# Modulation quarters on GpSimd: one broadcast multiply and a fold in place of tile-by-tile multiply and add

## What is computed

```python
c_act = jax.nn.silu(c)
mod = c_act @ w_ada[l] + b_ada[l]                      # [1, 6 * 2048]
sh1, sc1, gt1, sh2, sc2, gt2 = jnp.split(mod[:, None, :], N_MOD, axis=-1)
h = _rmsnorm(x, norm1_g[l]) * (1.0 + sc1) + sh1
...
x = x + gt1 * mix
h = _rmsnorm(x, norm2_g[l]) * (1.0 + sc2) + sh2
x = x + gt2 * _conv_ffn(h, w_up[l], conv_w[l], conv_b[l], w_down[l])
# second block, with c_2 and w_ada_2 (3 * 2048 columns)
shift, scale, gate = jnp.split(mod, 3, axis=-1)
```

## Time and profile before

| what | value |
|---|---|
| three runs | 2760.07, 2768.75, 2771.41 us; median 2768.75 |
| profiled execution, span | 2768.1 us |
| its own time | not given apart; the span lies 0.65 us under the median of the runs |
| PE busy | 2643.3 us (95%), granted clock 0.965 |
| DVE busy | 1864.0 us (67%) |
| POOL busy | 1128.9 us (41%), 612 instructions |
| ACT busy | 1082.6 us (39%) |
| DMA | 568.49 MB, mean 205 GB/s |

### The profile page before, as it was taken

How to read it: one execution, slowest core, us unless ns; L and a number is a source line. 1 busy time by engine, 2 the same in 40 slices (tenths; PEclk the granted TensorE clock), 3 DMA queues, 4 the chain that set the end, 5 groups by cost and what they waited for, 6 DMA issues and landing times.

```text
span 2768.1 us, 47948 instructions
## 1 busy us (share of the span) xinstructions
PE 2643.3 (95%) x20992; PEld 2397.8 (87%) x20992; DVE 1864.0 (67%) x2268; ACT 1082.6 (39%) x1255; POOL 1128.9 (41%) x612
## 2 busy tenths in 40 slices
PE   5689989999999999999999999999999999999997
PEld 2268877778999999999999899989988898999996
DVE  1248863267988888888887775576446874786454
ACT  1133422144434444343446443444334444444353
POOL 0293011013899999999991475862000000000001
PEclk7689989899999999999999999999999999999998
DMA  8967647676877777777765776775767665666664
GB/s 314 321 180 187 183 153 256 221 230 191 228 218 240 240 240 240 240 243 244 243 221 138 190 194 201 209 209 171 183 193 187 161 174 179 172 168 168 183 185 120
DMA packets 759185, 568.49 MB, mean 205 GB/s; under 512 B 46497, under 2 KB 645665, under 8 KB 758849
## 3 DMA queue, kind: packets, MB, share of 16 engines
q1 hardware_dynamic: 758976, 565.42, 69.7%
HBM read 563.29 MB, written 2.10 MB: 204 GB/s over the span
## 4 chain that ended last, share of the span: by engine, by line
PE 80%; DMA 6%; POOL 6%; DVE 5%; ACT 1%; issue 1%; SPq 1%; DVEq 0%; POOLq 0%
PE bank L785 15%; PE bank L768 9%; PE bank L769 9%; PE bank L772 9%; PE bank L788 8%; PE bank L752 5%; PE bank L754 5%; PE bank L753 5%; PE bank L1009 2%; DMA ada<-w_ada 2%; PE bank L741 2%; PE bank L821 2%; PE bank L822 2%; PE bank L823 2%; POOL prod_e L625 1%; POOL prod L625 1%
## 5 line engine op out<-in xcount | busy, mean ns | idle before, releaser
L1737 DVE TENSOR_TENSOR w_low<-ring,w_high 128x2048 fp32r<-128x2048 f32 x388 | 951.2, 2452 | 341.9 <-ACT w_high L1337 334.8
L1337 ACT ACTIVATE w_high<-ring 128x2048 fp32r<-128x2048 f32 x388 | 738.5, 1904 | 368.7 <-DMA ring<-w_in 127.6
L768 PE MATMUL bank<-acts,w_high 128*128 128x256 f32 x2400 | 586.4, 285 | 0.0
L769 PE MATMUL bank<-acts,w_high 128*128 128x256 f32 x2400 | 583.6, 283 | 0.0
L785 PE MATMUL bank<-acts,w_high 128*128 128x512 f32 (+1 forms) x2064 | 502.3, 396 | 11.1 <-DVE acts L1804 6.4
L768 PEld LDWEIGHTS bank<-acts,w_high 128*128 128x128 f32 x2400 | 461.6, 192 | 1.1 <-issue 0.2
L769 PEld LDWEIGHTS bank<-acts,w_high 128*128 128x128 f32 x2400 | 461.7, 192 | 0.0
L785 PEld LDWEIGHTS bank<-acts,w_high 128*128 128x128 f32 (+1 forms) x2064 | 382.7, 190 | 89.9 <-DVE acts L1804 6.5
L625 POOL TENSOR_SCALAR prod<-adf,cact 128x512 f32<-128x512 f32 x165 | 378.8, 2296 | 22.2 <-DMA adf<-w_ada 6.1
L639 POOL TENSOR_TENSOR sumf<-sqf 128x256 f32<-128x256 f32 x1 | 0.7, 743 | 789.7 <-ACT sqf L1718 789.7
L772 PE MATMUL bank<-acts,w_low 128*128 128x256 f32 x2400 | 312.4, 283 | 0.0
(11 more groups left out here) (457 smaller groups left out, 3711.2 us busy)
## 6 DMA issues: line engine op xcount, KB each, us to landing
ring<-w_in SPq DMA_DIRECT2D x182, 1024.0 KB, 5.8
ring<-w_up SPq DMA_DIRECT2D x88, 1024.0 KB, 5.9
ada<-w_ada SPq DMA_DIRECT2D x76, 1024.0 KB, 6.2
adf<-w_ada SPq DMA_DIRECT2D x44, 1024.0 KB, 8.1
ring<-w_down SPq DMA_DIRECT2D x44, 1024.0 KB, 6.4
ring<-w_out SPq DMA_DIRECT2D x16, 1024.0 KB, 6.0
adg<-w_ada SPq DMA_DIRECT2D x64, 256.0 KB, 5.6
ring<-w_mla SPq DMA_DIRECT2D x16, 1024.0 KB, 5.5
```

Source lines behind the costliest of these rows:

```text
L768: pe.matmul(o, wh[:, j], AH[:, j, :], start=j == 0, stop=False, skip_group_check=True)
L769: pe.matmul(o, wh[:, j], AL[:, j, :], start=False, stop=False, skip_group_check=True)
L1337: act.activation(WH[s][:, 0:WIDE[n]], ring[s][:, 0:WIDE[n]], ACT.Copy).then_inc(high_done, 1)
L1737: v.tensor_tensor(WL[s][:, 0:WIDE[n]], ring[s][:, 0:WIDE[n]], f32(WH[s][:, 0:WIDE[n]]), ALU.subtract)\
```

## The change

Per quarter, GpSimd now multiplies all four tiles (128x2048) in place by four columns of `cact`, each broadcast over 512 elements, in one TENSOR_TENSOR. It then adds the upper half to the lower half (128x1024), then the two remaining tiles (128x512), and that to `acc` (128x512). In the first quarter of a turn the second fold writes `acc` itself, so there are three instructions instead of four. The scratch tiles `prod_e` and `prod2` go.

```diff
-            def quarters(k, acc, prod, first):
+            def quarters(k, acc, first):
 
                 for q in range(4):
                     pool.wait_ge(f_landed[k % 2], 16 * (k // 2 + 1))
                     w = (AE if k < 4 * N_FIRST else AF)[k % 2][:, :].rearrange("p (j n) -> p j n", j=4)
-                    for j in range(4):
-                        col = cact[:, first + 4 * q + j:first + 4 * q + j + 1]
-                        if q == j == 0:
-                            ins = pool.tensor_scalar(acc[:, :], w[:, j, :], col, None, ALU.mult)
-                        else:
-                            after(pool.tensor_scalar(prod[:, :], w[:, j, :], col, None, ALU.mult))
-                            ins = pool.tensor_tensor(acc[:, :], prod[:, :], acc[:, :], ALU.add)
-                        if j < 3:
-                            after(ins)
+                    c = cact[:, first + 4 * q:first + 4 * q + 4].unsqueeze(2).broadcast_to([P, 4, 512])
+                    after(pool.tensor_tensor(w, w, c, ALU.mult))
+                    after(pool.tensor_tensor(w[:, 0:2, :], w[:, 0:2, :], w[:, 2:4, :], ALU.add))
+                    if q == 0:
+                        ins = pool.tensor_tensor(acc[:, :], w[:, 0, :], w[:, 1, :], ALU.add)
+                    else:
+                        after(pool.tensor_tensor(w[:, 0, :], w[:, 0, :], w[:, 1, :], ALU.add))
+                        ins = pool.tensor_tensor(acc[:, :], w[:, 0, :], acc[:, :], ALU.add)
                     k += 1
                     ins.then_inc(f_free, 1)
                     pool.wait_ge(f_free, k)
```

More of the change, by code:

```diff
@@ L239, in program @@
         acc_e = [at(f"acc_e{k}", W0 + 80 + 2 * k, [P, 512]) for k in range(2)]
-        prod_e = at("prod_e", W0 + 86, [P, 512])
         AG = [at(f"adg{k}", W0 + 100 + 2 * k, [P, 512]) for k in range(2)]
@@ L246, in program @@
         acc2 = [at(f"acc2{b}", W0 + 106 + 2 * b, [P, 512]) for b in range(2)]
-        prod2 = at("prod2", W0 + 70, [P, 512])
         BH = at("mix_high", W0 + 32, [P, 8, T], F32R)
@@ L644, in _ @@
             for t, (block, _) in enumerate(FIRST_TURNS):
-                quarters(4 * t, acc_e[t], prod_e, DT * block)
+                quarters(4 * t, acc_e[t], DT * block)
             pool.wait_ge(bonus_go, 1)
@@ L668, in _ @@
                     pool.wait_ge(ada_full, N_EARLY + 1 + turn - 1)
-                quarters(4 * (N_FIRST + turn), acc2[turn % 2], prod2, 0 if turn < 4 else DT)
+                quarters(4 * (N_FIRST + turn), acc2[turn % 2], 0 if turn < 4 else DT)
             for s in range(2):
```

## The result

The changed kernel takes 2939.7 us (median of four runs, 2933.76 to 2945.78), the kernel before 2768.53 beside it. The ratio is 1.0623, 95% interval 1.0601 to 1.0645. The profiled execution took 2934.87 us, its span 2933.1. The forecast was 2941, range 2835 to 2990.

The account below looks back on a forecast made before the run. TensorE runs without gaps mid-FFN, VectorE is slower in up units, and GpSimd's two-input instructions hold VectorE. FFN 156 + second norm 9 + first projection 10 - gains 2 = +173 us on 2768.1, so 2941 us; range 2835 to 2990.

Parts of the forecast that it names:

- What the change costs VectorE in the FFN: Ten full FFN turns: each of 40 quarters keeps VectorE waiting 3.9 us more, +156 us.
- the hold: Per FFN quarter, four GpSimd instructions each hold VectorE for their length less 0.15 us: 7.9 us, against 4.0 before.
- The pairs and the turn: FFN: a pair of up units goes from 12.35 to 16.25 us, a turn from 69.5 to 85.1 us.
- the signs that I gave: Expected in the profile: POOL busy falls, `hfu` and `hid_low` medians rise or spread, 16 us between `hfu`, turns of 85 us.
- The second norm: Ahead of the FFN: seven GpSimd instructions of 15.7 us meet a chain of short VectorE instructions; net +9 us.
- The first projection: Before TensorE's start at 129.84: seven GpSimd instructions stand ahead, 12.8 us of waits instead of 2.8, +10 us.
- The gains: After SP's wait of 200.73: the load leaves earlier and TensorE's idle time for a late `w_low` goes, -2 us.
- The port is let go: Rival: four GpSimd instructions hold VectorE under 4.0 us a quarter, so the change gains; 2750 us, chance 0.07.
- The multiply lets go: Rival: only the multiply lets VectorE go, the rest holds 4.5 us a quarter; 2768 us, no change, chance 0.05.
- My own rule: On GpSimd, a TENSOR_SCALAR holds VectorE only for its first third of a microsecond.
- Absorbed: Rival: VectorE's 10.6 us of idle time per FFN turn takes up the waits, turns grow 5 us; 2835 us, chance 0.16.
- Half held: Rival: the multiply holds VectorE for half its length, +96 us; 2864 us, chance 0.06.

Follow-up runs that it names:

- the kernel with the moved quarters: The change, with SP loading an FFN turn's four quarters one after each of the last down unit and the next turn's first three up units; 2854.44 us.
- The one-input version: The change with its broadcast multiply put back to four in-place TENSOR_SCALAR of 512 columns, the fold by halves kept; 2774.82 us.
- the multiply in four: The change with its broadcast multiply cut into four TENSOR_TENSOR of 512 columns; 2891.26 us.
- two of 1024: The change with its multiply as two TENSOR_SCALAR of 1024 columns, each by one column of c; 2775.7 us in one run.

## Why the prediction was right, point by point

**What the change costs VectorE in the FFN** was the main term, 156 us, and is 147.5. The length of the multiply was put at 3.59 us from the broadcast row of 1024 and is 3.60. The Trainium skill's figure for a plain add of 2048 (GPSIMD Engine Reference, Performance versus the Vector engine), 4497 ns, would have made it 0.9 us too long; the trace has no plain one. The step that was a little off is the hold: 7.9 us a quarter was predicted, 6.9 measured (291 / 42), and before 4.0 against 3.3 (140 / 42). Each of the 157 instructions of GpSimd's quarters in this stretch does hold one of VectorE. But the sum took four for every quarter where a turn's first has three, which is 11 us too much over ten turns, and VectorE's instruction mostly starts 0.1 to 0.2 us after GpSimd's. Both sides were too high, and the errors cancel in part: 3.9 was forecast for the difference and 3.6 came, which carries the 9 us. That the two-input multiply holds for its length less 0.15 us stands: the one above let go 0.13 before its end.

**The sum.** It was +173 us on the profiled execution and +165 came, so the 2941 beside a median of 2939.7 looks closer than the working was. Measured less forecast, the terms missed by -9 (FFN), +5 (second norm), +2 (first projection) and -5 (gains). TensorE also won 6.4 us of which the sum knew nothing, and lost 5 in small pieces between and after the stages. That these cancel to 8 us is in part luck.

**The pairs and the turn.** A turn of 85.1 us was forecast and 84.4 came. The way there is different. I spread a quarter over each pair (16.25 us each), while the quarters come at TensorE's pace and VectorE's pairs stretch, so that two pairs take nearly two quarters each (21.1 and 22.8) and the rest almost none. The sum is the same, since all four lie in the up units, as predicted. Of the signs that I gave, the 16 us between two `hfu` failed, and so did a higher median: that of `hfu` fell from 1.40 to 0.43 us. The spread came, with single ones at 3.7. Fewer instructions are held, each for longer.

**The second norm** was put at +9 us and is +14 (1.6 to 15.5). VectorE's short instructions there are held as forecast. That the granted clock in the 57 us around it was 0.84, where it was 0.94 before, wasn't in the sum.

**The first projection** was +10 and is +12. Seven instructions of GpSimd stand ahead of TensorE's start, as written; the eight scaling instructions took 16.9 us instead of 5.35.

**The gains** were 2 us and are 7 between matmuls 352 and 2000. SP's waits for the early quarters fell from 62 us to 18. Not all of it need be the change's: the kernel with only the early turns changed has the same instructions and waits there and gains 3, at a granted clock of 0.75 from 142 to 200 us, where the change had 0.85.

**Not foreseen** are 6.4 us that TensorE wins between matmuls 4800 and 5240, where no part of the change works. Before, its granted clock was 0.71 from 529 to 558 us; in the changed kernel it was 0.88 in that place. In the kernel with the moved quarters, the same up to there, it was 0.70 again. The thirteen traces know two lengths of this stretch, 21.4 to 23.0 us and 29.1 to 29.8. Of the seven kernels whose first projection starts 116.9 us or more after the first matmul six have the shorter one; the six that start at 115.1 or earlier all have the longer. So the same instructions can give either, and whether the change's later start makes the shorter one likelier stays open.

**The rivals.** *The port is let go* is out: the multiply's hold is seen directly, and doubling it costs 3.3 us each. *The multiply lets go* alone is out by the same. The rule of the Trainium skill that I quoted against the trace (SBUF — State Buffer, SBUF: two separate sides), the exclusive lock for the whole instruction, does not hold for a TENSOR_SCALAR of 512, which lets go 1.1 us before its end. For one of 2048 it is true but for the last 1.9 us, or the last 0.26 against VectorE's own TENSOR_SCALAR. The one-input version holds VectorE for 157 us, not far from the 140 of the kernel before, and that is why it is within 0.4% of it. My own rule, a third of a microsecond whatever the length, was too wide: it was read from 512 alone. It mattered to no term. *Absorbed* is out: held time is absorbed up to 140 to 160 us in the FFN, and before stood at 140 already. What the rival took for idle time, 10.6 us a turn, exists, but lies behind the burst. *Half held* is out by the hold.

**Open.** The versions with the multiply in four and with two of 1024 lie some 15 us below what their held time gives beside the change (275 against 291, but 902 us against 933; 173 and 800). Held time alone doesn't tell why.

## What to carry to other kernels

When work is moved between forms on GpSimd, count what it keeps VectorE from and not what GpSimd needs: a two-input instruction there costs VectorE its length, a short TENSOR_SCALAR a fraction of it and a long one most of it, and short pieces cost less than long ones, since the engines take turns. An engine that nobody waits for gains nothing by getting faster. And look at where a burst of holds falls against the buffers in between: here four ring slots covered two quarters, and the idle time came too late.

## What the runs showed of the hardware

- By the profile's times, whose ends on GpSimd are rough, GpSimd lets VectorE go 0.12 to 0.27 us before the end of a two-input instruction, for 256 to 2048 columns and whatever VectorE's instruction is. It lets go 1.0 to 1.15 us before the end of a TENSOR_SCALAR of 512 columns (0.26 in 4 of 117 cases in the kernel before, where VectorE's own TENSOR_SCALAR started in its last 0.55 us) and 1.9 to 2.0 us before that of one of 1024. Of one of 2048 it lets a two-input instruction of VectorE go 1.9 us before the end, and VectorE's TENSOR_SCALAR 0.26.
- An instruction of VectorE is held by one instruction of GpSimd at most: 0.58 us at the longest where GpSimd works in pieces of 256 columns, 3.4 us where it works in ones of 2048 with two inputs.
- A TENSOR_TENSOR with a broadcast input is the quicker one on GpSimd: 1.04 us for 512 columns and 3.60 for 2048, against 1.56 and 5.44 for a TENSOR_SCALAR, and 1.26 for 512 with two full inputs. The form that is faster by itself is the one that costs this kernel 6%.
- VectorE's sum of a PSUM and an SBUF tile is never held (0.69 us at the longest). The TENSOR_SCALAR of the convolution, from SBUF to SBUF with scalars beside it, is: it takes up to 3.8 us with the change instead of 0.41, and 5.5 beside the TENSOR_SCALAR of 2048.
